# The order of two accumulating matmuls inside one call of a gated-delta scan

## The reference

```python
def step(state, inp):
    u_i, wk_i, attn_i, q_i, k_i, gl_i = inp
    v_new = u_i - wk_i @ state
    o_i = q_i @ state + attn_i @ v_new          # the two products in question
    state = state * exp(gl_i) + einsum('bhcd,bhce->bhde', k_i, v_new)
    return state, o_i

for d in range(2):                              # forward, and backward on the flipped sequence
    state = zeros(heads, 128, 128)
    for stream in (context, latent):
        o, state = scan(step, state, chunks of stream)
        out[stream] += flip(o, d)               # only the latent stream's output is used
```

## Time and profile before

| | |
|---|---|
| median of 3 runs | 4606.37 us (4603.76 to 4617.8) |
| profiled execution, its own time | 4606.37 us |
| its span, first to last instruction | 4604.7 us |
| mean granted PE clock over the span | 0.889 |
| PE busy | 3666.0 us, 80% |
| calls of `outputs` | 16; first start of L2661 3778.9, last start of L2663 3984.8 |
| the lines of `outputs`, L2661 and L2663 | 256 matmul records each |

### The profile page before, as it was taken

How to read it: one execution, slowest core, us unless ns; L and a number is a source line. 1 busy time by engine, 2 the same in 40 slices (tenths; PEclk the granted TensorE clock), 3 DMA queues, 4 the chain that set the end, 5 groups by cost and what they waited for, 6 DMA issues and landing times. The chain is left out here.

```text
span 4604.7 us, 63969 instructions
## 1 busy us (share of the span) xinstructions
PE 3666.0 (80%) x28084; PEld 2875.9 (62%) x28084; DVE 2212.8 (48%) x2148; ACT 644.3 (14%) x980; POOL 796.6 (17%) x818
## 2 busy tenths in 40 slices
PE   7599999999989893599999999754665456785394
PEld 1277777777877782488788888542454345674183
DVE  0367777733335533554533533454777553314733
ACT  0022222211000001011110100111222112210001
POOL 0001111110000000051033250003727673000000
PEclk9799999999999996799999999866777778986697
DMA  7355555555334323322332334245465598651222
GB/s 260 106 157 149 154 155 147 151 168 157 106 102 131 123 96 137 59 76 82 97 90 86 101 109 124 98 158 164 137 195 168 163 206 193 199 186 38 73 101 110
DMA packets 679642, 611.47 MB, mean 133 GB/s; under 512 B 163952, under 2 KB 580776, under 8 KB 671056
## 3 DMA queue, kind: packets, MB, share of 16 engines
q1 hardware_dynamic: 556144, 403.55, 31.2%
q10 hardware_dynamic: 101296, 108.43, 7.1%
q0 software_dynamic: 21936, 95.56, 6.4%
HBM read 471.67 MB, written 135.82 MB: 132 GB/s over the span
## 5 line engine op out<-in xcount | busy, mean ns | idle before, releaser
L361 PE MATMUL front_ps<-b_hT,front_wb 128*128 128x512 f32 x4224 | 979.4, 392 | 18.7 <-DVE front_wb L351 18.7
L1251 PE MATMUL in_ps<-b_hT,in_wb 128*128 128x512 f32 (+3 forms) x4992 | 957.7, 354 | 10.7 <-DVE in_wb L1238 10.7
L1251 PEld LDWEIGHTS in_ps<-b_hT,in_wb 128*128 128x128 f32 (+1 forms) x4992 | 816.7, 188 | 158.4 <-issue 17.1
L361 PEld LDWEIGHTS front_ps<-b_hT,front_wb 128*128 128x128 f32 x4224 | 789.9, 188 | 199.6 <-DVE front_wb L351 22.1
L1236 DVE CAST in_wb<-in_raw 128x2048 fp32r<-128x2048 f32 (+1 forms) x68 | 82.7, 1216 | 562.0 <-PE in_ps L1251 541.5
L349 DVE CAST front_wb<-front_raw 128x2048 fp32r<-128x2048 f32 x88 | 108.0, 1227 | 434.2 <-PE front_ps L361 425.3
L755 POOL DMA_DIRECT2D front_mwb<-in_w_ada x128 | 101.2, 795 | 804.3 <-PE front_mps L765 801.6
L1086 PE MATMUL wout_ps<-wout_wb,wout_pair 128*128 128x512 f32 x768 | 177.4, 393 | 62.6 <-DVEq L1107 61.9
L1086 PEld LDWEIGHTS wout_ps<-wout_wb,wout_pair 128*128 128x128 f32 x768 | 145.5, 190 | 94.9 <-issue 64.6
L351 DVE TENSOR_TENSOR front_wb<-front_raw,front_wb 128x2048 fp32r<-128x2048 f32 x88 | 201.8, 2293 | 3.0
L1003 PE MATMUL merge_ps<-merge_pair,merge_wb 128*128 128x512 f32 x768 | 176.7, 393 | 22.3 <-DVEq L1021 22.3
(11 more groups left out here) (408 smaller groups left out, 4854.3 us busy)
## 6 DMA issues: line engine op xcount, KB each, us to landing
front_raw<-in_w_in SPq DMA_DIRECT2D x88, 1024.0 KB, 6.8
in_raw<-in_w_in SPq DMA_DIRECT2D x67, 1024.0 KB, 5.6
front_mwb<-in_w_ada POOLq DMA_DIRECT2D x128, 512.0 KB, 5.0
r_scr<-rprep_ob ACTq DMA_DIRECT2D x16, 2694.0 KB, 14.5
scan_rops<-r_scr SPq DMA_DIRECT2D x24, 1796.0 KB, 11.0
mod_wb<-in_w_ada SPq DMA_DIRECT2D x8, 4096.0 KB, 12.7
g_scr<-gprep_ob ACTq DMA_DIRECT2D x8, 3474.0 KB, 13.0
wo_raw<-in_w_o SPq DMA_DIRECT2D x16, 1024.0 KB, 5.0
```

Of the source, the lines that this page charges most:

```text
L361: last = self.nc.tensor.matmul(self.ps[:, n % 2, :], self.wb[:, n % 2, x, kt, :], self.hT[:, y, kt, :], start=kt == term == 0, stop=kt == ...
L1251: last = self.nc.tensor.matmul(self.ps[0:width, n % 3, first:end], self.wb[:, n % 2, x, kt, 0:width], self.hT[:, y, kt, first:end], start= ...
```

## The change

In `outputs` the loops over the two directions are merged. Before, a head's first products of both directions were issued one after the other, and then its second products of both directions. After, direction 0 gets its first and its second product, and then direction 1 gets its two. The matmuls themselves, their operands, their start and stop flags and the semaphore on the last one are the same.

```diff
-        rows = [slice(64 * d, 64 * d + 64) for d in range(2)]
         for h in range(H):
-            o = [self.po[r, h * GD:(h + 1) * GD] for r in rows]
             for d in range(2):
-                self.nc.tensor.matmul(o[d], self.chan[:, u, d, H * g + h, C:2 * C], self.state[:, g, d, h, :], start=True, stop=False)
-            for d, r in enumerate(rows):
-                last = self.nc.tensor.matmul(o[d], self.tok[r, u, H * g + h, 0:C], self.y[r, g, h, :], start=False, stop=True)
+                r = slice(64 * d, 64 * d + 64)
+                o = self.po[r, h * GD:(h + 1) * GD]
+                self.nc.tensor.matmul(o, self.chan[:, u, d, H * g + h, C:2 * C], self.state[:, g, d, h, :], start=True, stop=False)
+                last = self.nc.tensor.matmul(o, self.tok[r, u, H * g + h, 0:C], self.y[r, g, h, :], start=False, stop=True)
         last.then_inc(self.s["o_ok"], 1)
```

## The result

The changed kernel takes 4647.82 us (median of 4 runs) against 4610.26 for the kernel before beside it: a ratio of 1.008, 95% interval 1.0059 to 1.0099, so 27 to 46 us slower, 37 in the middle. The profiled execution took 4654.4 us, with a span of 4652.5; it is slower than each of the four runs of the median (4642.4 to 4650.0), so its trace shows some 10 us more of a difference than the medians do. A second series gave 1.008 again (1.0063 to 1.0097), with a span of 4647.9 in its trace. The lines of `outputs` are L2661 (state product) and L2662 (local product) now, and those behind it have moved up by one.

A forecast was written before the change was run, and what follows sets the result against it. TensorE (PE), busy 80% of the span, was taken as the bound. 7.5 us before and through its idle stretch, plus 28.3 for ten later calls, minus 4.2 of gaps, gave +31.6 on 4606.4: 4638.0 us, range 4618 to 4650.

The forecast's parts named there:

- A lone step: In `outputs`, one matmul standing alone between two changes of shape takes 0.36 us, a call 5.78 us instead of 2.95.
- Rival A: In `outputs`, matmuls wait only for those sharing their array part: +0.4 us per call, about 4610; 12 in 100.
- In front of the hole: Output steps 4 to 6, before PE's 22.70 us nearly idle stretch: 17 us added, 7.5 come through.
- the waits of L2632 for loads in steps 6 and 7: PE's load waits of 1.87 and 1.80 us would go, taking 3.7 us of the 17 added before the idle stretch.
- the wait at the hole: PE's wait at L2807 for the second scan's first inverses: some 16 us instead of 22.7, ending near 3855.
- the wait for a load that the forecast subtracted: Ahead of step 6's keys: 1.87 us of PE waiting for a load, taken off the calls' added time.
- Behind the hole: Steps 7 to 11, after PE's idle stretch: ten calls add 28.3 us, less 4.2 us of shorter instruction waits.
- The term for the gaps of "issue": PE's waits for code in steps 7 to 11: slower calls shorten three, 4.2 us back, bounds 0 and 8.
- the hole's delay: PE's idle stretch ends later, the second scan's inverses landing late behind load(8): 7.5 us, bounds 2 and 12.
- Rival B: In the calls PE's clock falls to 1.2 GHz: 4 us more per call, 40 for ten, 4678; 5 in 100.

The follow-up runs named there:

- alternating_lone: Kernel before, but each head issues direction 0's state and local product, then direction 1's local and state product (nine shape changes per call): ratio 1.0004.
- early_only: Kernel before with the changed order in output steps 4 to 6 alone, the old order in steps 7 to 11: 4625.83 us, ratio 1.002.
- warm_filler2: Changed kernel plus 56 additional 128 by 128 matmuls of a constant on PE ahead of step 4's keys: ratio 1.010 to the kernel before.
- late_only: Kernel before with the changed order in output steps 7 to 11 alone, the old order in steps 4 to 6: 4640.6 us, ratio 1.0055.
- grouped: Kernel before, pairs kept, but each call issues all four heads' state products first, then all their local products: ratio 0.9979.

## Why the prediction held, and what was off

**A lone step** was forecast at 0.36 us, a call at 5.78; they measure 0.36 and 5.77. Each call is +2.83 us, as worked out. The reading behind it (the change of shape costs, neither accumulation nor the number of matmuls) is shown by the table: over seven orders the time follows the changes and the steps of 0.22 us, and the extra time vanishes where no shape changes. One detail of it was wrong: a matmul is not alone because of the order, but because a change of shape stands on either side.

**Rival A** fell by the first trace: B0 and A1 lie in different column halves, and still start one after the other. `alternating_lone` shows what A would have looked like: 3.3 us.

**In front of the hole** the mechanism was right: the waits of L2632 for loads in steps 6 and 7 are gone, the inverses stand in the queue behind a later load(8), and the hole ends later. The size was off: 14 and 10 us in two traces where 7.5 were forecast. 9.6 and 5.5 of these are the later issue of the inverses, where the forecast had SP reach them only 1.5 us later, and 4.4 and 4.5 their longer way behind load(8). That the wait at the hole came out as forecast (15.1 and 15.7 us, forecast 16) is luck: PE reached it at 3846.2 and 3841.8, not at 3838, and its end was late as well. In the second trace steps 4 and 5 last 22.9 us each (call starts at 3778.2, 3801.1, 3824.0), where 21.1 (15.4 + 5.7) and 19.8 (15.9 + 5.7 - 1.9) follow from the forecast. About 1.5 us of each are the clock in the keys and values behind the calls: L2646 took 2.53 and 3.51 us there, where step 4 of the kernel before had 1.96. And the wait for a load that the forecast subtracted (1.87 us, ahead of step 6's keys) gave little back, because it had covered a wait for VectorE's update of the state, which stands in its place in the second trace:

```profile
3818.22 1.10 PE L2632 MATMUL scan_gwork<-scan_gstate,scan_gchan 128*64 128x128 f32 x16 [1.92 <-DVEq L2746]
```

In the first trace step 4's two calls alone cost 8.2 us more (9.87 instead of 5.77 each). That the low clock met step 4 there is chance: it began with the wait of 4.59 us ahead of the calls. Between executions the delay varies with the start of step 4 and with the solver's store, down to nothing in the traces of early_only and warm_filler2.

**Behind the hole** +28.3 - 4.2 = +24.1 us was forecast. late_only measures +25 (19 to 31) by its time. The term for the gaps of "issue" was about right: they shrank by 3.5 us in the first trace and 5.4 in late_only's, where 4.2 were expected. In the trace of the kernel after the stretch is 32.6 us longer: 28.3 for the calls at the full clock, less 3.5 of gaps, leaves 7.8. One call of step 8 at 1.2 GHz (9.87 us) makes 4.1 and the first call of step 10 makes 1.8 (8.90, less a gap of 1.33 inside and 5.77); the kernel before had 1.1 of the same kind (its call from 3945.42 took 6.73 us, less a gap of 2.72 and 2.94), so the calls account for 4.8. I put the other 3.0 down to other matmuls at the low clock, such as the state products behind that call of step 8 (2.08 us instead of 1.16).

The trace of warm_filler2 shows the sum without the clock. All ten calls behind its hole take 5.8 us, its gaps of "issue" are 19.1 us, and from the hole's end to the last state product it needs 163.9 us at a granted clock of 0.93, the clock of the kernel before. That is 25.0 us more than before, where 28.3 for the calls less 3.2 of gaps make 25.1:

```profile
3862.60:4026.50 163.90, 143.58 (x2850) 111.56 (x2852) 49.59 (x76) 35.93 (x75) 6.08 (x20) 0.93 0.61 166
```

A single trace has a scatter of some us here: the old order took 138.9 us for this stretch in the trace of before and 144.1 in that of early_only, at a granted clock of 0.88.

So two terms of the sum were mis-sized in the traces of the change: the clock, and the hole's delay, in part through the clock. **Rival B** was priced for all ten calls, with 5 in 100, and I set it at nothing otherwise; in the traces it takes one or two calls behind the hole, sometimes step 4, and some keys and values. 4638.0 is 10 us below the measured median, which lies inside the range (4647.8 of 4650). Of those 10 us, 4 are the level of the runs compared (before at 4610.3, not 4606.4). The other 6, 37.5 less 31.6, go the way of the clock and the later hole, but the interval of 27 to 46 us holds the forecast's 31.6 as well, so the times alone do not tell them from noise. The range held with 2 us to spare at its top, and the execution of the first trace lay above it.

What stays open: why the clock stays at 1.2 GHz through whole calls, in the old order too; why the solver's store and step 4 start earlier in one execution than in another; and whether the gaps of "issue" are code fetches; they behave as such, but nothing here tests it.

`grouped` beats both kernels: 0.9979 of before (0.997 to 0.9988), some 10 us, which answers to the 0.9 us per call and a hole that hides the first six. It needs only the order and the flags.

## What to carry to other kernels

Between two matmuls that use the array in different shapes there is a price (0.14 to 0.15 us here at 2.4 GHz, for 128 moving columns of float32), even where they lie in different column halves; so sort small matmuls by shape, and count the changes and not only the matmuls. Only three shapes were met here: 128 by 64, 64 by 64, and 64 by 128 behind a call. Neighbours of one shape in different column halves run side by side in either order. A wait that hides a slowdown can move itself: look at what stands in the same queue ahead of the transfer that ends it.

## What the runs showed of the hardware that was not expected

In one shape, A0, B0, A1, B1 issued in that order runs as two streams, one for each column half, started mostly within 0.01 to 0.06 us of each other at 0.22 us per step; A1, issued third, starts before B0, issued second. Where the shape changes between them, starts follow the order of issue. The Trainium skill (TensorEngine Tiling (Array Packing), Key Properties) says both that a change of the tiling mode drains TensorE and that tiles operate independently; the traces agree with both, and put 0.14 to 0.15 us on the first.

PE can be busy without a break and stay at 1.2 GHz: in step 4 of the first trace no idle time stands between 3770.23 and 3800.39, PE is busy for 23.90 of the 23.90 us of the calls' stretch, and the granted clock is 0.50 throughout. Four calls of sixteen lone steps were at 1.2 GHz from end to end (9.87 us instead of 5.77). It is no matter of the lone order: a call of the old order in early_only's trace was too, with 4.99 us instead of 2.94. Nor is it a rule: a call in the second trace of the changed kernel began at 1.2 GHz (3949.11), rose in its first step and took 5.92 us.

```profile
3979.40:3984.39 4.99, 4.99 (x37) 2.35 (x33) 0.00 (x0) 1.50 (x4) 0.00 (x0) 0.50 0.79 138
```

A call that began at 2.4 GHz kept it where no gap of "issue" stood just ahead of it or inside it. With a gap it did not always: in the second trace of the changed kernel PE waited 2.43 us on "issue", and the next call slowed down in its fourth step:

```profile
3933.72 0.28 PE L2617 MATMUL scan_gpx<-scan_gmid,scan_ginv 32*32 32x32 f32 x5 [2.43 <-issue]
...
3935.25 0.43 PE L2661 MATMUL scan_go<-scan_gstate,scan_gchan 128*64 128x128 f32 x2
3935.61 0.55 PE L2662 MATMUL scan_go<-scan_gy,scan_gtok 64*64 64x128 f32 x2
3936.09 0.69 PE L2661 MATMUL scan_go<-scan_gstate,scan_gchan 128*64 128x128 f32 x2
```
